# A two-block network on one core: the residual leaves SBUF during each expert loop, VectorE branches right behind the selection, and the second router's weights are loaded later

## The reference, cut to what matters

```python
def hier_moe(h, rg_w, rg_b, re_w, re_b, w_gate, w_up, w_down):
    ...
    gp = jax.nn.softmax((ht @ rg_w + rg_b).astype(jnp.float32), axis=-1)
    g_idx = jnp.argmax(gp, axis=-1)
    ...
    el = (ht @ re_w + re_b).astype(jnp.float32).reshape(T, N_GROUPS, EXPERTS_PER_GROUP)
    el = jnp.take_along_axis(el, g_idx[:, None, None], axis=1)[:, 0]
    top_p, top_i = lax.top_k(jax.nn.softmax(el, axis=-1), TOP_K)
    gates = g_prob[:, None] * top_p / jnp.sum(top_p, axis=-1, keepdims=True)
    ...
    order = jnp.argsort(flat_e, stable=True)
    ...
    def expert_block(args):
        xr, e = args
        return (jax.nn.silu(xr @ w_gate[e]) * (xr @ w_up[e])) @ w_down[e]
    ...
    out = jnp.zeros((T, D), jnp.float32).at[row_tok].add(y * row_w[:, None])

def first_block(x, ...):
    for l in range(DEPTH):                       # DEPTH = 2
        if l < N_A:
            x = x + pool_mixer(rms_norm(x, pool_norm[l]), ...)
        else:
            ...
            x = x + mla_attention(rms_norm(x, attn_norm[j]), ...)
        x = x + hier_moe(rms_norm(x, ffn_norm[l]), ...)
```

## Time and profile before

| | us |
|---|---|
| three runs, median (lowest to highest) | 1736.15 (1732.27 to 1739.38) |
| the profiled execution's own time | 1743.09 |
| span of its instructions on the core | 1741.3 |
| PE busy in the span (share) | 1630.9 (94%) |
| DVE busy (share) | 450.9 (26%) |
| ACT busy (share) | 235.8 (14%) |
| DMA ring in the first expert loop, from 100 to 560 us: share busy | 0.98 |

### The profile page before, as it was taken

The page is one execution under the profiler, slowest core; times in us unless marked ns, Lnnn a source line. Parts: engine busy times, 40 slices in busy tenths (PEclk is TensorE's granted clock), DMA queues, the critical chain, the costliest instruction groups (busy, mean ns, idle before and its releaser), DMA issues.

```text
span 1741.3 us, 22316 instructions
## 1 busy us (share of the span) xinstructions
PE 1630.9 (94%) x9137; PEld 1015.1 (58%) x9137; DVE 450.9 (26%) x971; ACT 235.8 (14%) x521; POOL 97.4 (6%) x165
## 2 busy tenths in 40 slices
PE   7999988899989999999988888989999998999998
PEld 7755544444446757645444444448577767688843
DVE  4311111111113324131111111124976211144411
ACT  4111000000002121100000000021123012100000
POOL 2300000000000000193000000010000000000000
PEclk9999999999999999999999999998999999999999
DMA  8999999999997442899999999996333541354300
GB/s 313 340 374 426 426 426 426 426 426 427 426 418 291 159 169 98 304 409 425 426 427 425 426 426 426 427 378 221 111 130 113 192 137 58 124 163 161 145 24 24
DMA packets 107045, 508.24 MB, mean 292 GB/s; under 512 B 16906, under 2 KB 46187, under 8 KB 73963
## 3 DMA queue, kind: packets, MB, share of 16 engines
q1 hardware_dynamic: 104699, 502.05, 72.1%
q10 hardware_dynamic: 2288, 5.40, 0.8%
HBM read 504.28 MB, written 3.15 MB: 291 GB/s over the span
## 4 chain that ended last, share of the span: by engine, by line
PE 39%; DMA 16%; DVE 4%; ACT 1%; issue 0%; DVEq 0%; ACTq 0%
DMA ring<-in_w_up 16%; PE PS L1379 9%; PE PS L885 6%; PE PS L1145 4%; PE PS L1389 4%; PE PS L1156 2%; PE PS L928 2%; PE PS L1320 2%; PE PS L1309 2%; PE PS L1332 2%; PE PS L914 1%; DVE arena L2183 1%; PE PS L1357 1%; PE PS L830 0%; PE PS L704 0%; DVE XN L2282 0%
## 5 line engine op out<-in xcount | busy, mean ns | idle before, releaser
L885 PE MATMUL PS<-ring,arena 128*64 128x256 f32 x4032 | 462.1, 384 | 68.3 <-DMA ring<-in_w_up 50.4
L885 PEld LDWEIGHTS PS<-ring,arena 128*64 128x64 f32 x4032 | 291.0, 138 | 260.4 <-DMA ring<-in_w_up 69.5
L928 PE MATMUL PS<-ring,arena 128*64 128x512 f32 x1024 | 233.8, 598 | 1.2 <-ACT arena L1556 1.2
L2001 DVE TENSOR_TENSOR arena<-PS,arena 128x256 f32<-128x256 f32 x64 | 27.2, 425 | 737.6 <-ACT arena L1548 737.6
L928 PEld LDWEIGHTS PS<-ring,arena 128*64 128x64 f32 x1024 | 68.2, 136 | 157.9 <-issue 157.9
L1379 PE MATMUL PS<-hT,ring 128*128 128x256 f32 x704 | 152.1, 379 | 0.0
L1379 PEld LDWEIGHTS PS<-hT,ring 128*128 128x128 f32 x704 | 133.7, 190 | 18.1
L914 PE MATMUL PS<-arena,hT 64*128 64x512 f32 x512 | 127.2, 615 | 1.9 <-ACT arena L1565 1.9
L1145 PE MATMUL PS<-hT,ring 128*128 128x256 f32 x448 | 102.0, 390 | 0.0
L1145 PEld LDWEIGHTS PS<-hT,ring 128*128 128x128 f32 x448 | 87.4, 196 | 13.7 <-issue 1.5
L1556 ACT ACTIVATE arena<-PS 128x256 f32<-128x256 f32 x64 | 24.6, 384 | 517.8 <-PE PS L901 517.8
(11 more groups left out here) (399 smaller groups left out, 1375.0 us busy)
## 6 DMA issues: line engine op xcount, KB each, us to landing
ring<-in_w_up SPq DMA_DIRECT2D x64, 2048.0 KB, 25.6
ring<-in_w_down SPq DMA_DIRECT2D x64, 2048.0 KB, 24.6
ring<-in_w_gate SPq DMA_DIRECT2D x62, 2048.0 KB, 25.5
ring<-in_f_w_up SPq DMA_DIRECT2D x22, 1024.0 KB, 7.4
ring<-in_w_in SPq DMA_DIRECT2D x9, 2048.0 KB, 14.1
ring<-in_f_w_down SPq DMA_DIRECT2D x5, 2048.0 KB, 8.2
arena<-in_w_gate SPq DMA_DIRECT2D x2, 2048.0 KB, 22.8
ring<-in_x_wkv SPq DMA_DIRECT2D x2, 2048.0 KB, 7.9
```

What stands on the lines that cost most here:

```text
L885: mm = pe.matmul(PS[half * WINDOW:(half + 1) * WINDOW, bank, m * half_f:(m + 1) * half_f], xw[bank][:, k, :], mat[:, k, half * half_f:(hal ...
L928: mm = pe.matmul(PS[half * WINDOW:(half + 1) * WINDOW, 3, :], hidT[:, w, k * WINDOW:(k + 1) * WINDOW], mat[:, k, half * 512:(half + 1) * 5 ...
```

## The change

There are three parts.

**The residual and one more slab.** When X is ready, SP stores it to DRAM (`park_x`, 1 MB). When that store has landed and the norm has read X, SP loads slab 6 of the loop in two halves: one over X, one into a part of `arena` (`load_over_x`, `split`). So slabs 5 and 6 are both outside the ring (`AHEAD`, `SPLIT`), slab 7 takes the place that slab 6 had, slabs 8 to 12 take those of slabs 0 to 4, and from slab 13 on slab j takes the place of slab j-6. Behind the last slab of the loop SP loads X back (`fetch_x`), and VectorE waits for it before the addition. In layer 1 the half in `arena` lies over the memory's normed rows, so the load also waits for `slabs_done` to reach the loop's first slab. TensorE reads each row block of such a slab from the half that holds it (`piece`). Three small buffers move in `arena`.

**VectorE's branch.** The wait, the load of the largest count and the branch now follow `sel` directly. The eight products (`spread`) come behind the first window, the slot numbers (`window_slots`) and the reciprocal behind the second. The first window's start is 0 and is written into the instruction.

**The second router's weights.** `loads_ahead` loses its wait and moves in SP's queue from the first loop's start into latent attention, between the loads for the memory's values and those of `wo`.

```diff
-AHEAD = (MOE0 + 5, MOE1 + 5)
+AHEAD = (MOE0 + 5, MOE0 + 6, MOE1 + 5, MOE1 + 6)
+SPLIT = (MOE0 + 6, MOE1 + 6)
+AHEAD_BYTES = 16 * 3
...
+        split = [[X[:, :, :].rearrange("p t d -> p (t d)"), ar(at, half_slab)] for at in (17984, 12288)]
...
             def loads_ahead():
-                sp.wait_ge(s["route_max"], 1)
                 router_loads(1)
...
+                def park_x():
+                    sp.wait_ge(s["x_ready"], MOE_X[layer])
+                    sp.dma_start(x_park, X[:, :, :]).then_inc(s["x_loaded"], 16)
+                def load_over_x():
+                    name = ("ffn0", "ffn1")[layer]
+                    sp.wait_ge(s["x_loaded"], 16 * (2 + 2 * layer))
+                    sp.wait_ge(s["norm_xn"], TT * (SCALED.index(name) + 1))
+                    sp.wait_ge(s["norm_turned"], 4 * (TURNED.index(name) + 1))
+                    if layer == 0:
+                        sp.wait_ge(s["norm_turned"], 4 * (TURNED.index("mem") + 1))
+                        sp.wait_ge(s["route_max"], 1)
+                    else:
+                        sp.wait_ge(s["slabs_done"], n0)
+                    m, e = expert_slab(RING)
+                    src = (gate, up)[m][e]
+                    for i, dst in enumerate(split[layer]):
+                        sp.dma_start(dst, src[:, i * half_slab:(i + 1) * half_slab]).then_inc(s["ahead_loaded"], 16)
+                def fetch_x():
+                    sp.dma_start(X[:, :, :], x_park).then_inc(s["x_loaded"], 16)
...
+                park_x()
                 if layer == 0:
                     load_ahead()
-                    loads_ahead()
-                for j in range(first + 1, 2 * RING):
+                load_over_x()
+                for j in range(first + 2, 3 * RING):
                     placed(j)
...
+                fetch_x()
...
+            loads_ahead()
             for half in range(2):
                 rows(MLA0 + 8 + half, a["wo"][0][:, half * 512:(half + 1) * 512], HEADS, 512)
...
-                    second = after((0, 0), 0)
-                    start_0, start_1 = load_start((0, 0)), load_start(second[0])
+                    steps[0] = at_branch
                     sorted_out(0)
                     dve.wait_ge(s["pad_ready"], q + 1)
                     sorted_wait(0)
-                    window((0, 0), 0, start_0)
-                    window(*second, start_1)
+                    window((0, 0), 0, 0)
+                    spread()
+                    if windows == 1:
+                        window((0, 1), 0)
+                    else:
+                        window((0, 0), 1, 0)
+                    window_slots(step_dve)
...
+                dve.wait_ge(s["x_loaded"], 16 * (3 + 2 * layer))
                 for t in range(TT):
                     dve.tensor_tensor(X[:, t, :], X[:, t, :], PS[:, 4 + 2 * t:6 + 2 * t, :].rearrange("p b n -> p (b n)"), ALU.add)\
```

More of the change, by code:

```diff
@@ L376, in program, with piece @@
         ahead = ar(8192, SLAB)
+        half_slab = SLAB // 2
+        split = [[X[:, :, :].rearrange("p t d -> p (t d)"), ar(at, half_slab)] for at in (17984, 12288)]
+        def piece(n, k, width):
+            if n in SPLIT:
+                each = half_slab // width
+                return split[SPLIT.index(n)][k // each][:, k % each * width:(k % each + 1) * width]
+            return slab(n)[:, k * width:(k + 1) * width]
         band = ar(0, N_POOL, BAND)
@@ L605, in experts @@
                         m, e = expert_slab(RING + k)
-                        one(n0 + RING + k, m, i * BODY + (e - BODY), loaded(n0 + RING + k))
+                        one(n0 + 2 * RING + k, m, i * BODY + (e - BODY), loaded(n0 + 2 * RING + k))
                 for j in range((turns - 1) * RING, EXPERT_SLABS):
                     placed(j)
+                fetch_x()
             wkv = a["x_wkv_2"][0]
@@ L857, in view @@
                         turn = e[0] if isinstance(e[0], int) else 1
-                        return slab(n0 + turn * RING + e[1] * PER_EXPERT + plus)
+                        n = n0 + turn * RING + e[1] * PER_EXPERT + plus
+                        return lambda k, width: piece(n, k, width)
                     def place(e, plus):
@@ L929, in down @@
                                                hidT[:, w, k * WINDOW:(k + 1) * WINDOW],
[L930 removed]
+                                               mat(k, D)[:, half * 512:(half + 1) * 512], start=(k == 0), stop=(k == KF - 1))
                         mm.then_inc(s["slabs_done"] if w == windows - 1 else g["y"], 1)
@@ L1945, in moe, with spread, window_slots @@
                         last.then_inc(s["select_ready"], 1)
-                for i, v in enumerate((pos, gat)):
-                    for k in range(TOP_K):
-                        for t in range(TT):
-                            last = dve.tensor_scalar(diag[:, i, k * TT + t, :], ident, v[:, k, t, :], None, ALU.mult)
-                last.then_inc(s["select_ready"], 1)
-                for w in range(WINDOWS):
-                    dve.tensor_scalar(slot_of[:, w, :], incl, cc("row_1")[:, w:w + 1], None, ALU.add)
-                    last = dve.tensor_scalar(slot_valid[:, w, :], cnt, cc("row")[:, w:w + 1], None, ALU.is_gt)
-                step(last)
-                step(dve.tensor_tensor(slot_of, slot_of, slot_valid, ALU.mult))
-                step(dve.tensor_scalar(slot_of, slot_of, 1.0, None, ALU.subtract))
-                if layer == 0:
-                    dve.wait_ge(s["s5_th"], 2)
-                    dve.reciprocal(den, den).then_inc(s["s5_small"], 1)
+                def spread():
+                    for i, v in enumerate((pos, gat)):
+                        for k in range(TOP_K):
+                            for t in range(TT):
+                                last = dve.tensor_scalar(diag[:, i, k * TT + t, :], ident, v[:, k, t, :], None, ALU.mult)
+                    last.then_inc(s["select_ready"], 1)
+                def window_slots(step):
+                    for w in range(WINDOWS):
+                        dve.tensor_scalar(slot_of[:, w, :], incl, cc("row_1")[:, w:w + 1], None, ALU.add)
+                        last = dve.tensor_scalar(slot_valid[:, w, :], cnt, cc("row")[:, w:w + 1], None, ALU.is_gt)
+                    step(last)
+                    step(dve.tensor_tensor(slot_of, slot_of, slot_valid, ALU.mult))
+                    step(dve.tensor_scalar(slot_of, slot_of, 1.0, None, ALU.subtract))
+                    if layer == 0:
+                        dve.wait_ge(s["s5_th"], 2)
+                        dve.reciprocal(den, den).then_inc(s["s5_small"], 1)
+                at_branch = steps[0]
                 dve.wait_ge(s["fgain_loaded"], 16)
@@ L1993, in window @@
                             start = load_start(e)
-                        dve.tensor_copy(xw[(e[1] * windows + w) % 2], xs[:, :, bass.ds(start + w * WINDOW, WINDOW)])\
-                           .then_inc(g["window"], 1)
+                        if isinstance(start, int):
+                            rows = slice(start + w * WINDOW, start + (w + 1) * WINDOW)
+                        else:
+                            rows = bass.ds(start + w * WINDOW, WINDOW)
+                        dve.tensor_copy(xw[(e[1] * windows + w) % 2], xs[:, :, rows]).then_inc(g["window"], 1)
                     def hids(e, w):
```

22 lines of the change are left out of this document (11 added, 11 removed).

## The result

| | before | after | ratio (95% interval) |
|---|---|---|---|
| median, us (lowest to highest) | 1736.62 (1732.27 to 1739.38) | **1727.07** (1725.45 to 1727.89) | 0.994 (0.9922 to 0.9958) |
| both once more (`after_again` below) | 1737.78 (1731.91 to 1740.65) | 1728.22 (1725.96 to 1729.44) | 0.9948 (0.9932 to 0.9963) |
| profiled execution, us | 1743.09 | 1725.45 | |

What follows compares the result with a forecast made beforehand. DMA was taken to bound the expert loops from about slab 13, PE their start and the attention. Layer 0's 4.70 us plus layer 1's 5.16, less 0.3, gave 9.6: from the 1736.15 median to 1726.6, range 1718 to 1738.

Steps and rivals of the forecast that it cites:

- DMA's queue from slab 13 on sets the loop's end: Expert loops: DMA is full from about slab 13, so the end is that slab's issue plus 83 slabs.
- Part 1, the start: First expert of each layer: VectorE's earlier branch lets PE start 3.18 us sooner in layer 0, 2.26 in layer 1.
- What was to be late next: Ahead of the first expert: PE's own keys in layer 0 and ScalarE in layer 1 would then set the start.
- Part 1, the clock: First expert's gate and up: clock stays at 1.00 with less idle time, gaining 1.52 and 2.90 us; bounds 0 and 4.42.
- The row at 29.50 in the earlier trace: PE idle in the middle of a shorter pause with clock 1.00, taken as a sign that the clock would stay up.
- Part 2, the slab: Expert loops: one more slab outside the ring gains 0; bounds 0 and 5.1 us in each loop.
- Part 2, X's trip: Attention behind the first loop: reading X back delays the keys' weights, costing 0.3 us; bounds 0 and 2.6.
- Part 3: Router loads moved into the attention: they delay only `wo`, read when the attention has finished; 0 us.
- Code late on PE: Rival, PE's branch in layer 0: late code leaves the start unchanged, 4.9 us gained, 1731.3 us; chance 0.18.
- The slower case: Rival, PE's branch in layer 0: code waits for several blocks behind a full queue, 2.7 us slower, 1738.8; chance 0.10.
- the slab in full: Rival, both expert loops: the extra slab saves 5.1 us in each, 19.8 us in all, 1716.4; chance 0.07.
- the clock did not fall in layer 1: Rival, layer 1's first expert: the clock falls all the same, 6.7 us gained, 1729.4; chance 0.08.

Runs made afterwards that it cites:

- after_again: The changed kernel once more, in more runs beside VectorE's new order alone on the same chip: 0.9948 of before, median 1728.22 us.
- e1_again: The kernel before with only VectorE's new order, run once more on the same chip as the changed kernel: 0.9952 of before, median 1728.89 us.
- e1_branch_only: The kernel before with only VectorE's new order around its branch: 0.9952 of before, 8.3 us faster.
- e2_slab_only: The changed kernel with VectorE's order put back as before (X parked, extra slab and moved router loads kept): 1.0015 of before, 2.6 us slower.
- e3_clock: The kernel before with 20 unused matmuls filling TensorE's idle time ahead of its branch in both layers: 1.0003 of before.
- e3b_clock_half: The kernel before with 10 unused matmuls ahead of TensorE's branch in each layer: 1.0004 of before.

## Why the prediction was right, and which terms were mis-sized

**DMA's queue from slab 13 on sets the loop's end.** Right, and more exactly than was claimed: 421.4 to 421.5 us from that issue to the addition in all four loops of before and after, and 421.2 to 422.9 in the twelve loops of `after_again`, `e1_again`, `e1_branch_only`, `e2_slab_only`, `e3_clock` and `e3b_clock_half`. A start moved by PE moves the end one for one, within 1.7 us.

**Part 1, the start.** Forecast 3.18 and 2.26; PE's idle time fell from 3.18 to 0 and from 3.57 to 1.25, so 3.18 and 2.32. What was to be late next was: PE's keys in layer 0, ScalarE in layer 1. VectorE's slack in layer 0 was larger than 1.6: its window began at 55.71, and with 0.68 for PE's start it would have let PE go at 56.4, 2.6 ahead. The products at 56.05 cost nothing.

**Part 1, the clock.** In the profiles 1.52 and 2.90 came back, as forecast: the first `gate_up` takes 7.13 us in both layers in all nine profiles with VectorE's new order. The row at 29.50 in the earlier trace rows was weak ground for it, since in that same execution the clock fell at 37, seven us later. As a term of the medians 4.42 was too large. It was read from one execution, whose mean granted clock was 0.986; before's runs lie between 0.987 and 0.994, and are 1739.5 to 1742.0 us at 0.987 and 1732.2 to 1733.0 at 0.994 on one chip. That not every execution of before loses the clock at these two places, so that not every one can win it back, fits this but is not shown: there is one profile of before. The measured gain of 8.3 to 9.6 us less 5.5 for the starts leaves 3 to 4, `e3_clock` says 1.5 to 2.2 with a wide interval, and the runs at equal clock say 1 to 2.5. The clock's part of the medians is thus some 2 us, between 1 and 4, of the 4.42. That the sum still came out within 0.5 us of the median is in part luck: the clock's term was some 2 us too large, and the parts that can be sized add up to 1 to 2 us less than the 9.6 measured (5.5 for the starts, some 2 for the clock, 0.6 to 1.1 for the slab, less 0.2).

**Part 2, the slab: 0.** Right but for 0.6 to 1.1 us. The pause that spoke for it before (0.71 and 0.83 in the earlier trace rows) became a stop of 6.3 us (forecast 8). The loops are 0.2 and 0.9 us shorter than in `e1_branch_only`, and 0.2 and 0.4 in the second pair of profiles, which is all that the slab brought.

**Part 2, X's trip: 0.3.** The rows say 0.22 (4.44 against 4.22), and `e1_branch_only`, without the trip, has the 4.22 of before (526.28 less 522.06). In `e2_slab_only`, with the trip, the keys come 4.53 us behind the addition, and the row names the weights that the forecast named:

```profile
531.18 3.72 PE L765 MATMUL PS<-arena,ring 128*128 128x256 f32 x16 [0.16 <-DMA ring<-in_x_wkv]
```

Nothing shows a cost of the store or of the wait for X.

**Part 3: 0** in this kernel. In `e1_branch_only` DMA moves only 164 and 139 GB/s from 56 to 64 us, where the router loads run; that is before slab 13, and so hidden. In the attention the loads hold SP's issue for 3.47 and 3.14 us at most, not for 18. What they would cost in a kernel without a pause ahead of slab 13 no run shows.

**The rivals.** Code late on PE did not come: in layer 0 PE has no idle time. The Trainium skill (Runtime: NRT & Kernel Launch, Instruction fetch mechanics) has a taken branch wait for a DMA of its target where that isn't in the window already fetched; VectorE's 5.84 and 2.74 agree, PE's rows in the changed kernel don't show it. `e3b_clock_half` shows that PE can stop for 2.39 us behind its branch; whether for this reason is open. The slower case did not come for the same reason, the slab in full fell by `e2_slab_only`, and the clock did not fall in layer 1 (1.00, 7.13 us).

## What to carry to other kernels

Where a queue is full for most of a loop, look for the last place at which it was not. What moves that issue moves the end, one for one, and a buffer gained ahead of it is worth next to nothing unless it is still occupied then: against VectorE's order alone, which has slab 5 outside the ring, two places outside it brought about 1 us with slabs 5 and 6 (the loops' lengths), and 12 us with slabs 18 and 19 (0.9952 less 0.988). A term read from one profiled execution (here the clock) is a term of that execution; set its mean clock against those of the other runs before adding it to a median.

## What was not expected of the hardware

The time of one kernel follows its mean granted clock: over 29 runs of before on one chip it falls by about 1.1 us for each 0.001 more, from 1742.0 at 0.987 to 1732.2 at 0.994. The falls stand at different places in different executions: at 36 to 46 us (0.66) and in both first `gate_up` in before's profile, in the attention in those of `e2_slab_only` and `e3_clock` (0.83 over 10 us), most of them right behind an idle time of PE, the one at 37 us seven us after one. `e1_branch_only` has the same idle times in the attention (628 to 632 us) and keeps a clock of 1.00 there. Why the same idle time goes with a fall in one execution and not in another is open.

PE can stop in the middle of a run of matmuls for 2.39 us with no wait in the profile (`e3b_clock_half`, layer 1, 697 to 699). And VectorE's time behind a taken branch was 5.84 us where DMA was full (share 1.01) and 2.74 where it was idle (0.03); before it was 6.1 and 2.9.
